# The end of a hybrid layer kernel: the last 64 tokens on all 128 partitions, and GpSimd as a third engine for the last block

## Chip, cores and metric

The kernel runs on one core of one Trainium2 chip. The metric is the device time of one execution in microseconds; lower is better. Three runs of the kernel before have a median of 1894.53 us.

## What is computed

One step of a one-layer streaming encoder, in fp32, for 320 tokens (64 of a sample, 256 of a prompt) of 2048 features: a projection, two attention mixers, a gated merge, a channel mixer with 8192 hidden features, a gated per-layer embedding and a final normalisation. Only the last two matter here:

```python
def rmsnorm(x, g):
    y = x32 * lax.rsqrt(jnp.mean(x32 * x32, axis=-1, keepdims=True) + RMS_EPS)
    return (y * g.astype(jnp.float32)).astype(x.dtype)
...
    gate = jax.nn.sigmoid(rmsnorm(h, g_ple) @ w_ple_gate)
    return h + (ple.astype(h.dtype) @ w_ple_proj) * gate
...
    y_prompt = rmsnorm(hp, g_final)
    y_sample = rmsnorm(hs, g_final)
```

## The kernel before

Activations lie transposed: features on the 128 partitions in 16 blocks (`KB`), 320 tokens (`TOK`) in the columns of each block. Every weight matrix comes as slabs of 8 x 128 x 128 over the SP queue, is split into a high and a low part by ACT (L628) and DVE (L947), and is multiplied in three passes (L394 to L396). The order on each engine is that of the code, with semaphores written out by hand.

The last matrix is the gate of the per-layer embedding, one block of 128 features after another. For each block, DVE scales the bank (L1131), ACT takes the sigmoid (L804), DVE multiplies by the projected embedding (L1245) and adds it to `h` (L1247); GpSimd squares the block (L1337) and adds it to `ssq` (L1340), and ACT multiplies `h` by the final gain (L913). The last block has code of its own, in two halves of 160 tokens: DVE L1258, ACT L922, then DVE L1262 (product), L1264 (sum) and L1269 (square). ACT loads the table of the square root meanwhile (L643) and scales the block by the gain (L925).

Then the result is turned into rows. TensorE sums the squares over the partitions for three groups of 128 tokens, 0 to 127, 128 to 255 and 192 to 319 (L596 for `ssq`, L604 for the last block's `sq`). ACT takes the root (L928), DVE the reciprocal (L1271). A "piece" is 128 tokens by 512 features: four transposes into a bank (L588), then a scaling by the reciprocal root out of the bank into `y_rows`, even pieces on ACT (L935), odd ones on DVE (L1278). There are five banks for pieces, and four pieces are transposed before the sums are known. The third group has only 64 new tokens. They come out on partitions 64 to 127 of their banks, and their pieces are scaled and stored as 64 rows. Two pieces make a store of 1024 features on the SP queue (L362): six stores, those of 128, 128 and 64 rows for the first half of the features, then the same for the second. SP waits for both engines' count of pieces before each, and at the end for all stores.

Two earlier transfers on ACT's queue are spoken of too. L747 copies a table from DRAM to DRAM into `bias_rows`, which is 1024 rows of 1 KB; L748 and L749, the `rolled` outputs, follow it as 16 pieces of 16 KB each. L774 and L775 each store 8 rows:

```python
act.dma_start(bias_rows, bass.AP(tensor=rel.tensor, offset=P - 1, ap=[[BIAS_ROW, HEADS], [-1, P], [1, 2 * P]])).then_inc(s_brow, 16)
act.dma_start(f_rows, f_sum[0:HEADS, :]).then_inc(s_fst, 16)
act.dma_start(io["logf_t"], logf[:, PAST:KEYS]).then_inc(s_out, 16)
```

The first view is (stride, count) by dimension, the outermost first: 8 heads, 128 rows, 256 elements. L963, also spoken of, is DVE's low part of an input block, `x_lo`, from `h` and `x_hi`.

## Time and profile before

| what | value |
|---|---|
| median of three runs | 1894.53 us (1893.93 to 1895.15) |
| the profiled execution, its own time | 1894.25 us |
| its span | 1892.4 us |
| TensorE busy | 1882.9 us |
| moved by DMA | 292.36 MB, mean 154 GB/s |

The span runs from the first to the last record of the profiled execution, and its own time is 1.85 us longer. All rows are from that one execution, in microseconds from the start of the span. PE is the matmul engine, DVE, ACT and POOL (GpSimd) are the others, SPq and ACTq are the queues of transfers that SP and ACT issue. A DMA share of 1.00 means that all 16 DMA engines of the core are busy (it can read a little over 1).

### The profile page before, as it was taken

The page shows a single profiled execution, that of the slowest core. Times are in us where ns is not written, and L with a number is a line of the kernel's source. Part 1 is how long each engine was busy: PE and PEld are TensorE (multiplying, and loading weights), DVE is VectorE, ACT ScalarE, POOL GpSimd, SP SyncE. Part 2 cuts the span into 40 slices and gives each one's busy share as a digit, 9 for nine tenths or more (in the row PEclk, how much of TensorE's full clock was granted, in tenths as well). Part 3 has the DMA queues.
Part 4 walks back from the last instruction along what each step waited for, and adds up shares of the span by engine and source line. Part 5 has one row for each costly group of instructions (what it writes and reads, how often), then busy time and mean ns, then how long its engine had stood idle before and what let it go on. Part 6 is the DMA issues. An engine that isn't in the chain of part 4 may idle for free.

```text
span 1892.4 us, 34998 instructions
## 1 busy us (share of the span) xinstructions
PE 1882.9 (99%) x12883; PEld 1879.1 (99%) x12883; DVE 894.3 (47%) x1122; ACT 726.8 (38%) x907; POOL 193.9 (10%) x280
## 2 busy tenths in 40 slices
PE   9999999999999999999999999999999999999998
PEld 9999999999999999999999999999999999999998
DVE  8544444444444444555443444444444344455544
ACT  6334443343333333334333333333333233333554
POOL 0111111120000000220100011000100001122121
PEclk9999999999999999999999999999999999999999
DMA  7544444546444444444444444444444444444442
GB/s 263 169 158 163 161 161 163 164 138 214 148 155 133 157 154 139 149 155 152 144 156 155 140 149 155 156 145 143 152 146 154 146 149 142 153 153 145 152 149 100
DMA packets 94306, 292.36 MB, mean 154 GB/s; under 512 B 13072, under 2 KB 26536, under 8 KB 94120
## 3 DMA queue, kind: packets, MB, share of 16 engines
q1 hardware_dynamic: 75760, 275.32, 44.3%
q10 hardware_dynamic: 18520, 16.69, 2.9%
q8 instruction: 17, 0.28, 0.1%
q14 instruction: 9, 0.07, 0.0%
HBM read 284.08 MB, written 9.46 MB: 155 GB/s over the span
## 4 chain that ended last, share of the span: by engine, by line
PE 99%; DVE 0%; DMA 0%; ACT 0%; issue 0%; SPq 0%; ACTq 0%
PE banks L394 31%; PE banks L396 31%; PE banks L395 31%; PE banks L470 0%; PE banks L471 0%; PE banks L472 0%; PE banks L416 0%; PE banks L419 0%; PE banks L417 0%; PE banks L568 0%; PE banks L566 0%; PE banks L567 0%; DMA h<-in_x_t 0%; PE banks L445 0%; PE banks L444 0%; PE banks L447 0%
## 5 line engine op out<-in xcount | busy, mean ns | idle before, releaser
L628 ACT ACTIVATE w_hi<-w_raw 128x1024 fp32r<-128x1024 f32 x510 | 539.7, 1061 | 996.4 <-PE banks L396 987.7
L394 PE MATMUL banks<-x_hi,w_hi 128*128 128x320 f32 x2512 | 780.6, 311 | 0.0
L396 PE MATMUL banks<-x_hi,w_lo 128*128 128x320 f32 x2512 | 776.2, 309 | 0.0
L395 PE MATMUL banks<-x_lo,w_hi 128*128 128x320 f32 x2512 | 776.1, 309 | 0.0
L947 DVE TENSOR_TENSOR w_lo<-w_raw,w_hi 128x1024 fp32r<-128x1024 f32 x510 | 605.0, 1222 | 23.7 <-ACT w_hi L628 23.6
L395 PEld LDWEIGHTS banks<-x_lo,w_hi 128*128 128x128 f32 x2512 | 471.8, 188 | 0.2
L394 PEld LDWEIGHTS banks<-x_hi,w_hi 128*128 128x128 f32 x2512 | 471.7, 188 | 0.2
L396 PEld LDWEIGHTS banks<-x_hi,w_lo 128*128 128x128 f32 x2512 | 471.6, 188 | 0.0
L394 PE MATMUL banks<-o_hi,w_hi 128*128 128x320 f32 x1280 | 395.6, 309 | 0.0
L396 PE MATMUL banks<-o_hi,w_lo 128*128 128x320 f32 x1280 | 395.5, 309 | 0.0
L395 PE MATMUL banks<-o_lo,w_hi 128*128 128x320 f32 x1280 | 395.5, 309 | 0.0
L394 PEld LDWEIGHTS banks<-o_hi,w_hi 128*128 128x128 f32 x1280 | 240.3, 188 | 0.0
L395 PEld LDWEIGHTS banks<-o_lo,w_hi 128*128 128x128 f32 x1280 | 240.3, 188 | 0.0
L396 PEld LDWEIGHTS banks<-o_hi,w_lo 128*128 128x128 f32 x1280 | 240.3, 188 | 0.0
L1174 DVE TENSOR_TENSOR h<-banks,h 128x320 f32 x80 | 39.4, 492 | 263.2 <-PE banks L396 263.2
L1348 POOL TENSOR_TENSOR tmp<-tmp 128x320 f32<-128x320 f32 x64 | 46.2, 722 | 741.5 <-DVE tmp L1188 741.5
L1188 DVE SCALAR_TENSOR_TENSOR tmp<-banks,rstd 128x320 f32<-128x320 f32 x64 | 31.5, 492 | 137.6 <-PE banks L396 137.6
L1337 POOL TENSOR_TENSOR sq<-h 128x320 f32 x47 | 33.9, 722 | 584.5 <-DVE h L1174 504.0
L1131 DVE TENSOR_TENSOR tmp<-banks,rstd 128x320 f32<-128x320 f32 x47 | 23.1, 491 | 126.6 <-PE banks L396 126.6
L1192 DVE TENSOR_TENSOR o_lo<-tmp,o_hi 128x320 f32 (+1 forms) x64 | 31.5, 492 | 104.7 <-ACT o_hi L860 103.4
L394 PE MATMUL banks<-m_hi,w_hi 128*128 128x320 f32 x256 | 79.1, 309 | 0.0
L395 PE MATMUL banks<-m_lo,w_hi 128*128 128x320 f32 x256 | 79.1, 309 | 0.0
(159 smaller groups left out, 1046.0 us busy)
## 6 DMA issues: line engine op xcount, KB each, us to landing
w_raw<-in_w_slabs SPq DMA_DIRECT2D x515, 512.0 KB, 4.1
out_kv_t<-k_t ACTq DMA_DIRECT2D x16, 160.0 KB, 3.7
out_kv_t<-v_t ACTq DMA_DIRECT2D x16, 160.0 KB, 4.4
h<-in_x_t ACTq DMA_DIRECT2D x1, 2560.0 KB, 10.2
out_y<-y_rows SPq DMA_DIRECT2D x4, 512.0 KB, 4.0
h<-in_x_t SPq DMA_DIRECT2D x3, 640.0 KB, 9.2
f_keys<-f_rows ACTq DMA_DIRECT2D x8, 224.0 KB, 3.1
bias_rows<-in_rel_rows ACTq DMA_DIRECT2D x1, 1024.0 KB
```

Of the source, the lines that this page charges most:

```text
L394: nc.tensor.matmul(out, w_hi[:, slot, ws], hi[:, xs], start=k == lo_k, stop=False)
L395: nc.tensor.matmul(out, w_hi[:, slot, ws], lo[:, xs], start=False, stop=False)
L396: mm = nc.tensor.matmul(out, w_lo[:, slot, ws], hi[:, xs], start=False, stop=k == hi_k)
L628: nc.scalar.activation(w_hi[:, slot, :], w_raw[:, slot, :], ACT.Copy).then_inc(s_whi, 1)
L947: nc.vector.tensor_tensor(w_lo[:, slot, :], w_raw[:, slot, :], f32(w_hi[:, slot, :]), ALU.subtract).then_inc(s_wlo, 1)
L1131: nc.vector.tensor_tensor(tm(dst), summed(t, base), rstd[:, :], ALU.mult).then_inc(s_acc, 1)
L1174: nc.vector.tensor_tensor(blk(h, n), summed(t), blk(h, n), ALU.add).then_inc(s_acc, 1)
L1188: nc.vector.scalar_tensor_tensor(out=tm(0), in0=acc, scalar=0.0, in1=rstd[:, :], op0=ALU.max, op1=ALU.mult).then_inc(s_acc, 1)
L1192: nc.vector.tensor_tensor(blk(o_lo, n), tm(1), f32(blk(o_hi, n)), ALU.subtract).then_inc(s_olo, 1)
L1337: nc.gpsimd.tensor_tensor(sq[:, :], blk(h, n), blk(h, n), ALU.mult).then_inc(s_sq, 1)
L1348: nc.gpsimd.tensor_tensor(tm(1), tm(0), tm(0), ALU.mult).then_inc(s_sqr, 1)
```

## The change

The third group of tokens gets all 128 partitions. For it, TensorE turns four blocks of the features' second half (all 128 columns, of which partitions 64 to 127 are wanted) and then, over partitions 0 to 63 of the same bank, the matching blocks of the first half for the 64 tokens alone. So there are ten pieces in place of twelve, all of 128 partitions by 512, and the third group is one store, whose target is seen as (half, token, feature). Its place is third, behind the first halves of the other groups. Since the token's reciprocal root is now wanted on partitions 0 to 63 too, DVE takes a second reciprocal that moves it there.

The last block is cut at 128 tokens in place of 160. GpSimd does product, sum and square for the first 128, DVE for the other 192, and GpSimd multiplies the whole block by the gain, which ACT did.

```diff
-Y_ROWS = ((0, 0, P), (P, 0, P), (TOK - P, P - (TOK - 2 * P), TOK - 2 * P))
+LAST_TOK = TOK - 2 * P
 Y_BLOCKS = 4
-Y_PIECES = tuple((rows, 2 * pair + e) for pair in range(KB // Y_BLOCKS // 2) for rows in range(len(Y_ROWS)) for e in range(2))
+HALF_KB = KB // 2
+Y_PIECES = ((0, 0), (0, 1), (1, 0), (1, 1), (2, 0), (2, 1), (0, 2), (0, 3), (1, 2), (1, 3))
+Y_COLS = (0, D_MODEL, 2 * D_MODEL)
...
-        def token_half(t, half):
-            return t[:, half * (TOK // 2):(half + 1) * (TOK // 2)]
+        def token_part(t, part):
+            return t[:, part * P:part * P + (P, TOK - P)[part]]
+        def tokens_of(t, rows, block=0):
+            last = block * TOK + min(rows * P + P, TOK)
+            return t[:, last - P:last]
         def y_piece(n, at_bank):
             rows, group = Y_PIECES[n]
-            first, at, count = Y_ROWS[rows]
-            cols = slice(group * Y_BLOCKS * P, (group + 1) * Y_BLOCKS * P)
+            first = Y_COLS[rows] + group * Y_BLOCKS * P
             if at_bank:
-                return banks[at:at + count, Y_BANKS[n % len(Y_BANKS)], 0:Y_BLOCKS * P]
-            return y_rows[at:at + count, rows * D_MODEL + cols.start:rows * D_MODEL + cols.stop]
+                return banks[:, Y_BANKS[n % len(Y_BANKS)], 0:Y_BLOCKS * P]
+            return y_rows[:, first:first + Y_BLOCKS * P]
...
-                first, at, count = Y_ROWS[rows]
                 cols = slice(group * Y_BLOCKS * P, (group + 2) * Y_BLOCKS * P)
-                src = y_rows[at:at + count, rows * D_MODEL + cols.start:rows * D_MODEL + cols.stop]
+                src = y_rows[:, Y_COLS[rows] + cols.start:Y_COLS[rows] + cols.stop]
+                dst = io["y"][rows * P:rows * P + P, cols] if rows < 2 else \
+                    io["y"][2 * P:TOK, :].rearrange("t (h c) -> h t c", h=2)
                 sp.wait_ge(s_scaled[0], pair + 1)
                 sp.wait_ge(s_scaled[1], pair + 1)
-                sp.dma_start(io["y"][first + P - count if at else first:first + P, cols], src).then_inc(s_stored, 16)
+                sp.dma_start(dst, src).then_inc(s_stored, 16)
...
             def turn_piece(n):
                 rows, group = Y_PIECES[n]
-                first = Y_ROWS[rows][0]
                 for j in range(Y_BLOCKS):
                     block = group * Y_BLOCKS + j
-                    src = h[:, block * TOK + first:block * TOK + first + P]
-                    tr = nc.tensor.transpose(banks[:, Y_BANKS[n % len(Y_BANKS)], j * P:(j + 1) * P], src, ident[:, :])
+                    out = banks[:, Y_BANKS[n % len(Y_BANKS)], j * P:(j + 1) * P]
+                    if rows < 2:
+                        tr = nc.tensor.transpose(out, tokens_of(h, rows, block), ident[:, :])
+                    else:
+                        nc.tensor.transpose(out, tokens_of(h, rows, block + HALF_KB), ident[:, :])
+                        tr = nc.tensor.transpose(out[0:LAST_TOK], tokens_of(h, rows, block)[:, P - LAST_TOK:P], ident[:, :])
                 tr.then_inc(s_turned_y, 1)
             ready_pieces = len(Y_BANKS) - 1
             pe.wait_ge(s_ssq, 3 * KB)
             row_sums = [banks[:, bank, 0:1] for bank in SUM_BANKS]
-            for out, (first, at, count) in zip(row_sums, Y_ROWS):
-                nc.tensor.matmul(out, ssq[:, first:first + P], ones[:, 0:1], start=True, stop=False)
+            for rows, out in enumerate(row_sums):
+                nc.tensor.matmul(out, tokens_of(ssq, rows), ones[:, 0:1], start=True, stop=False)
             pe.wait_ge(s_hg, KB - 1)
             for n in range(ready_pieces):
                 turn_piece(n)
-            for out, (first, at, count) in zip(row_sums, Y_ROWS):
-                pe.wait_ge(s_gated[3], 1 if first + P <= TOK // 2 else 2)
-                mm = nc.tensor.matmul(out, sq[:, first:first + P], ones[:, 0:1], start=False, stop=True)
+            for rows, out in enumerate(row_sums):
+                pe.wait_ge(s_squared[min(rows, 1)], 1)
+                mm = nc.tensor.matmul(out, tokens_of(sq, rows), ones[:, 0:1], start=False, stop=True)
             mm.then_inc(s_sum, 1)
             for n in range(ready_pieces, len(Y_PIECES)):
                 if n == len(Y_BANKS) - 1:
@@ -611,9 +626,9 @@
                     done = n - len(Y_BANKS)
                     pe.wait_ge(s_scaled[done % 2], by_engine(done + 1, done % 2))
-                if Y_PIECES[n][1] == KB // Y_BLOCKS - 1:
-                    pe.wait_ge(s_hg, KB)
+                if Y_PIECES[n] in ((0, 3), (1, 3), (2, 1)):
+                    pe.wait_ge(s_lasthg, 1)
...
-                nc.scalar.activation(token_half(tm(1), part), token_half(tm(0), part), ACT.Sigmoid).then_inc(s_gated[1], 1)
+                nc.scalar.activation(token_part(tm(1), part), token_part(tm(0), part), ACT.Sigmoid).then_inc(s_gated[1], 1)
             ready_root()
-            act.wait_ge(s_gated[3], 2)
-            nc.scalar.activation(blk(h, KB - 1), blk(h, KB - 1), ACT.Copy, scale=gain(FINAL, KB - 1)).then_inc(s_hg, 1)
             act.wait_ge(s_sum, 4)
             sums = banks[:, SUM_BANKS[0]:SUM_BANKS[-1] + 1, 0:1].rearrange("p b n -> p (b n)")
-            nc.scalar.activation(mean[:, 0:len(Y_ROWS)], sums, ACT.Sqrt, bias=eps[:, :], scale=1.0 / D_MODEL).then_inc(s_row_root, 1)
-            act.wait_ge(s_row_rstd, 1)
+            nc.scalar.activation(mean[:, 0:len(SUM_BANKS)], sums, ACT.Sqrt, bias=eps[:, :], scale=1.0 / D_MODEL).then_inc(s_row_root, 1)
             for n in range(0, len(Y_PIECES), 2):
                 rows = Y_PIECES[n][0]
-                first, at, count = Y_ROWS[rows]
+                if n == 0 or rows == 2:
+                    act.wait_ge(s_row_rstd, 1 + rows // 2)
                 act.wait_ge(s_turned_y, n + 1)
-                nc.scalar.activation(y_piece(n, False), y_piece(n, True), ACT.Copy, scale=rstd[at:at + count, rows:rows + 1]).then_inc(s_scaled[0], 1)
+                nc.scalar.activation(y_piece(n, False), y_piece(n, True), ACT.Copy, scale=rstd[:, rows:rows + 1]).then_inc(s_scaled[0], 1)
...
-                nc.vector.tensor_tensor(token_half(tm(0), part), token_half(acc, part), token_half(rstd, part), ALU.mult).then_inc(s_gated[0], 1)
-            for part in range(2):
-                dve.wait_ge(s_gated[1], part + 1)
-                nc.vector.tensor_tensor(token_half(tm(2), part), token_half(tm(1), part), token_half(blk(ple_part, n), part), ALU.mult).then_inc(s_gated[2], 1)
-                dve.wait_ge(s_gated[2], part + 1)
-                nc.vector.tensor_tensor(token_half(blk(h, n), part), token_half(blk(h, n), part), token_half(tm(2), part), ALU.add).then_inc(s_plep, 1)
-                dve.wait_ge(s_plep, KB + part)
-                if part == 0:
-                    dve.wait_ge(s_ssq, 3 * KB)
-                nc.vector.tensor_tensor(token_half(sq, part), token_half(blk(h, n), part), token_half(blk(h, n), part), ALU.mult).then_inc(s_gated[3], 1)
+                nc.vector.tensor_tensor(token_part(tm(0), part), token_part(acc, part), token_part(rstd, part), ALU.mult).then_inc(s_gated[0], 1)
+            dve.wait_ge(s_gated[1], 2)
+            nc.vector.tensor_tensor(token_part(tm(2), 1), token_part(tm(1), 1), token_part(blk(ple_part, n), 1), ALU.mult).then_inc(s_gated[2], 1)
+            dve.wait_ge(s_gated[2], 1)
+            nc.vector.tensor_tensor(token_part(blk(h, n), 1), token_part(blk(h, n), 1), token_part(tm(2), 1), ALU.add).then_inc(s_plep, 1)
+            dve.wait_ge(s_plep, KB)
+            dve.wait_ge(s_ssq, 3 * KB)
+            nc.vector.tensor_tensor(token_part(sq, 1), token_part(blk(h, n), 1), token_part(blk(h, n), 1), ALU.mult).then_inc(s_squared[1], 1)
             dve.wait_ge(s_row_root, 1)
-            nc.vector.reciprocal(rstd[:, 0:len(Y_ROWS)], mean[:, 0:len(Y_ROWS)]).then_inc(s_row_rstd, 1)
+            nc.vector.reciprocal(rstd[:, 0:len(SUM_BANKS)], mean[:, 0:len(SUM_BANKS)]).then_inc(s_row_rstd, 1)
             dve.wait_ge(s_row_rstd, 1)
+            nc.vector.reciprocal(rstd[0:LAST_TOK, 2:3], mean[LAST_TOK:P, 2:3]).then_inc(s_row_rstd, 1)
             for n in range(1, len(Y_PIECES), 2):
                 rows = Y_PIECES[n][0]
-                first, at, count = Y_ROWS[rows]
+                if n == 1 or rows == 2:
+                    dve.wait_ge(s_row_rstd, 1 + rows // 2)
                 dve.wait_ge(s_turned_y, n + 1)
-                nc.vector.tensor_scalar(y_piece(n, False), y_piece(n, True), rstd[at:at + count, rows:rows + 1], None, ALU.mult).then_inc(s_scaled[1], 1)
+                nc.vector.tensor_scalar(y_piece(n, False), y_piece(n, True), rstd[:, rows:rows + 1], None, ALU.mult).then_inc(s_scaled[1], 1)
         @block.gpsimd
@@ -1348,6 +1362,19 @@
                     nc.gpsimd.tensor_tensor(tm(1), tm(0), tm(0), ALU.mult).then_inc(s_sqr, 1)
             add_squares(1, s_acc, T_PLE - KB + 1)
             add_squares(2, s_hfin, 1, KB - 1)
+            n = KB - 1
+            pool.wait_ge(s_pread, 4)
+            pool.wait_ge(s_gated[1], 1)
+            nc.gpsimd.tensor_tensor(token_part(tm(2), 0), token_part(tm(1), 0), token_part(blk(ple_part, n), 0), ALU.mult).then_inc(s_gated[3], 1)
+            pool.wait_ge(s_gated[3], 1)
+            nc.gpsimd.tensor_tensor(token_part(blk(h, n), 0), token_part(blk(h, n), 0), token_part(tm(2), 0), ALU.add).then_inc(s_gated[3], 1)
+            pool.wait_ge(s_gated[3], 2)
+            nc.gpsimd.tensor_tensor(token_part(sq, 0), token_part(blk(h, n), 0), token_part(blk(h, n), 0), ALU.mult).then_inc(s_squared[0], 1)
+            for part in range(2):
+                pool.wait_ge(s_squared[part], 1)
+            nc.gpsimd.tensor_scalar(blk(h, n), blk(h, n), gain(FINAL, n), None, ALU.mult).then_inc(s_lasthg, 1)
```

On SP, the queue of stores, the end of the program read before:

```order
L330 DMA w_raw<-in_w_slabs 128x1024
L347 REGISTER_ALU
L347 COMPARE_AND_BRANCH
L362 DMA out_y<-y_rows 128x1024 [waits piece_scaled_vector,piece_scaled_scalar] x2
L362 DMA out_y<-y_rows 64x1024 [waits piece_scaled_vector,piece_scaled_scalar]
L362 DMA out_y<-y_rows 128x1024 [waits piece_scaled_vector,piece_scaled_scalar] x2
L362 DMA out_y<-y_rows 64x1024 [waits piece_scaled_vector,piece_scaled_scalar]
L124 UNCONDITIONAL_BRANCH [waits y_stored]
```

and reads now:

```order
L340 DMA w_raw<-in_w_slabs 128x1024
L357 REGISTER_ALU
L357 COMPARE_AND_BRANCH
L373 DMA out_y<-y_rows 128x1024 [waits piece_scaled_vector,piece_scaled_scalar] x2
L373 DMA out_y<-y_rows 2x64x1024 [waits piece_scaled_vector,piece_scaled_scalar]
L373 DMA out_y<-y_rows 128x1024 [waits piece_scaled_vector,piece_scaled_scalar] x2
L127 UNCONDITIONAL_BRANCH [waits y_stored]
```

Five stores stand where six stood, and the third has a target of three dimensions; its source is 128 partitions of 1024 elements.

On GpSimd, behind the loop that sums the squares, the program ended; now its end reads:

```order
L1351 TENSOR_TENSOR sq<-h 128x320
L1354 TENSOR_TENSOR ssq<-ssq,sq 128x320 [waits square_ready]
L1347 REGISTER_ALU
L1347 COMPARE_AND_BRANCH
L1369 TENSOR_TENSOR tmp<-tmp,ple_part 128x128 [waits last_block_gated1,ple_part_read]
L1371 TENSOR_TENSOR h<-h,tmp 128x128 [waits last_block_gated3]
L1373 TENSOR_TENSOR sq<-h 128x128 [waits last_block_gated3]
L1377 TENSOR_SCALAR h<-h,gains 128x320 [waits last_block_squared1,last_block_squared0]
L127 UNCONDITIONAL_BRANCH
```

Four operations are new there, each behind the one before it. On DVE the last block's part was two such triples:

```order
L1258 TENSOR_TENSOR tmp<-banks,rstd 128x160 [waits slab_multiplied]
L1258 TENSOR_TENSOR tmp<-banks,rstd 128x160
L1262 TENSOR_TENSOR tmp<-tmp,ple_part 128x160 [waits last_block_gated1]
L1264 TENSOR_TENSOR h<-h,tmp 128x160 [waits last_block_gated2]
L1269 TENSOR_TENSOR sq<-h 128x160 [waits square_sum_ready,ple_gated]
L1262 TENSOR_TENSOR tmp<-tmp,ple_part 128x160 [waits last_block_gated1]
L1264 TENSOR_TENSOR h<-h,tmp 128x160 [waits last_block_gated2]
L1269 TENSOR_TENSOR sq<-h 128x160 [waits ple_gated]
L1271 RECIPROCAL rstd<-mean 128x3 [waits row_roots_ready]
```

and is now one, with a second reciprocal behind it:

```order
L1272 TENSOR_TENSOR tmp<-banks,rstd 128x128 [waits slab_multiplied]
L1272 TENSOR_TENSOR tmp<-banks,rstd 128x192
L1275 TENSOR_TENSOR tmp<-tmp,ple_part 128x192 [waits last_block_gated1]
L1277 TENSOR_TENSOR h<-h,tmp 128x192 [waits last_block_gated2]
L1281 TENSOR_TENSOR sq<-h 128x192 [waits square_sum_ready,ple_gated]
L1283 RECIPROCAL rstd<-mean 128x3 [waits row_roots_ready]
L1285 RECIPROCAL rstd<-mean 64x1 [waits row_rstd_ready]
```

## Rows read from the trace of the kernel before

**Rows 1.** The page, parts 1 and 4: busy time, and the chain by engine

```profile
PE 1882.9 (99%) x12883; PEld 1879.1 (99%) x12883; DVE 894.3 (47%) x1122; ACT 726.8 (38%) x907; POOL 193.9 (10%) x280
...
PE 99%; DVE 0%; DMA 0%; ACT 0%; issue 0%; SPq 0%; ACTq 0%
```

**Rows 2.** Chain of waits at the end, in order of time: start us, us, what

```profile
1878.26 0.34 DVE tmp L1258
1878.62 0.35 ACT tmp L922
...
1880.67 0.34 DVE sq L1269
1881.05 0.62 PE banks L604 x4
...
1881.99 0.19 DVE rstd L1271
1882.20 0.70 ACT y_rows L935
...
1886.25 0.76 DVE y_rows L1278
```

**Rows 3.** Timeline of the SP queue, first and third store: start us, us, what

```profile
1883.03 0.35 SPq L362 DMA_DIRECT2D out_y<-y_rows  x1
...
1884.47 0.53 SPq L362 DMA_DIRECT2D out_y<-y_rows  x1
```

**Rows 4.** Windows of the tail: stretch, length, busy time by engine, PEclk, DMA share, GB/s

```profile
1883.75:1884.00 0.25, 0.25 (x5) 0.25 (x4) 0.25 (x1) 0.25 (x1) 0.00 (x0) 1.00 0.58 229
1884.00:1884.25 0.25, 0.25 (x5) 0.25 (x4) 0.25 (x1) 0.23 (x2) 0.00 (x0) 1.00 1.00 410
1884.00:1886.50 2.50, 2.21 (x21) 1.98 (x19) 2.14 (x4) 2.24 (x4) 0.00 (x0) 1.00 1.02 397
1886.50:1888.00 1.50, 0.00 (x0) 0.00 (x0) 0.51 (x1) 0.00 (x0) 0.00 (x0) 1.00 1.00 197
1891.25:1891.50 0.25, 0.00 (x0) 0.00 (x0) 0.00 (x0) 0.00 (x0) 0.00 (x0) 0.50 0.91 279
```

**Rows 5.** DMA view, 1883 to 1892 us: all packets of the six stores

```profile
DMA packets 736, 2.62 MB, mean 291 GB/s; under 512 B 96, under 2 KB 96, under 8 KB 736
```

**Rows 6.** DMA view, 52.2 to 54.1 us: queue 10, packets, MB, share

```profile
q10 hardware_dynamic: 32, 0.02, 6.6%
```

**Rows 7.** DMA view, 19 to 31.5 us: queue 10

```profile
q10 hardware_dynamic: 1096, 1.57, 41.1%
```

**Rows 8.** Timeline, 1872 to 1882 us, DVE, POOL and ACT

```profile
1872.78 0.49 DVE L1247 TENSOR_TENSOR h<-h,tmp 128x320 f32<-128x320 f32 x1
1873.54 0.72 POOL L1337 TENSOR_TENSOR sq<-h 128x320 f32 x1 [1.88 <-DVE h L1247]
...
1881.03 0.56 ACT L925 ACTIVATE h<-h,gains 128x320 f32<-128x320 f32 x1 [0.32 <-DVE sq L1269]
```

**Rows 9.** Groups of instructions by line and form: busy us, mean ns, idle before

```profile
L963 DVE SCALAR_TENSOR_TENSOR x_lo<-h,gains,x_hi 128x320 fp32r<-128x320 f32 x16 | 7.8, 550 | 1.3 <-ACT x_hi L722 1.3
L1247 DVE TENSOR_TENSOR h<-h,tmp 128x320 f32 x14 | 6.9, 493 | 1.7
L1264 DVE TENSOR_TENSOR h<-h,tmp 128x160 f32<-128x160 f32 x2 | 0.7, 326 | 0.1
L1340 POOL TENSOR_TENSOR ssq<-ssq,sq 128x320 f32<-128x320 f32 x47 | 41.4, 880 | 3.7
L1337 POOL TENSOR_TENSOR sq<-h 128x320 f32 x47 | 33.9, 722 | 584.5 <-DVE h L1174 504.0 <-DVE h L1247 80.5
L1313 POOL TENSOR_SCALAR probs<-probs,inv_sum 128x128 f32<-128x128 f32 x16 | 10.4, 648 | 285.8 <-DVE inv_sum L997 285.8
```

**Rows 10.** Timeline at 745 us: a GpSimd and a DVE operation at once

```profile
745.44 0.88 POOL L1340 TENSOR_TENSOR ssq<-ssq,sq 128x320 f32<-128x320 f32 x1
745.45 1.22 DVE L963 SCALAR_TENSOR_TENSOR x_lo<-h,gains,x_hi  x1 [1.09 <-ACT x_hi L848]
```

More of the change, by code:

```diff
@@ L148, in hybrid_layer @@
         wf = under("wf", [P, WF_COLS], F32R)
-        y_rows = under("y_rows", [P, len(Y_ROWS) * D_MODEL])
+        y_rows = under("y_rows", [P, 2 * D_MODEL + D_MODEL // 2])
         m_hi = sb("m_hi", [P, KB * TOK], F32R)
@@ L254, in hybrid_layer @@
         s_gated = [sem(f"last_block_gated{i}") for i in range(4)]
+        s_lasthg = sem("last_block_gained")
+        s_squared = [sem(f"last_block_squared{i}") for i in range(2)]
         s_root = sem("root_ready")
```

## The prediction

> **What bounds the kernel now.** Start with the busy shares and the chain that ended last: TensorE is busy for 1882.9 of 1892.4 us and holds 99% of the chain [rows 1]. Up to the last gate product at 1878.2 us nothing in the change touches anything, so the whole question lies in the last 14 us. There the chain in order of time [rows 2] shows a relay between DVE, ACT and PE: gate logits at 1878.26, sigmoid, product, sum and square in two halves of 160 tokens until 1881.01, row sums until 1881.67, root, reciprocal, and the first scaling at 1882.20. The SP queue's timeline [rows 3] shows the first of six stores issued at 1883.03, and the windows [rows 4] show its data flowing from about 1883.85 (a 0.58 share of the quarter from 1883.75) to about 1891.5. From there on the reader is to look at the DMA share, not at an engine: it stands near 1.00 all the way, while DVE and ACT are done at 1887.0. The tail is bound by the 16 DMA engines, 7.65 us of data, followed by 0.9 us to the end of the span.
>
> The windows also show two rates. With full stores running, 397 GB/s on average; in the stretch in which the first 64-partition store runs, 197 GB/s at the same busy share. So 256 KB from 64 partitions cost as much as 512 KB from 128: 512 KB at 410 GB/s, the best quarter [rows 4], are 1.28 us, and six stores are 6 x 1.28 = 7.68, which is the 7.65 read.
>
> **The change, part by part.**
>
> *Six stores become five.* Two stores of 64 partitions go, and one with 128 source partitions comes. The total is 2.62 MB, as before. If all 16 engines share it, it costs 1.28 us in place of 2.56.
>
> *How the new store is spread.* This is the term that decides. Its source is 128 partitions; its target is the view "h t c", whose outer dimension is 2, then 64 rows of 4 KB. The order rows show 2x64x1024 where all the others have 128x1024. How many engines share a store can be read from its completion packets of 4 bytes: one for each engine that took part. The six stores of the end left 96 of them, 16 each, for outer dimensions 128 and 64 [rows 5]. The two stores of 8 rows at 52 us (`f_rows`, `logf_t`) left 32 packets on queue 10 together: 16 rows of data and 16 completions, 8 each [rows 6]. The telling case is the copy into `bias_rows`: its target is 1024 rows, its source has an outer dimension of 8 and then 128. With the two `rolled` copies (16 pieces each) queue 10 moved 1096 packets: 1024 + 32 of data leaves 40 completions, 16 + 16 for `rolled` and 8 for `bias_rows` [rows 7]. The side with the small outer dimension decided, though the other side had 1024. A number of engines that divides both outer dimensions fits every one of these cases (16, 16, 8, 8), and for 128 against 2 it gives 2.
>
> The Trainium skill, "DMA: Bandwidth & Descriptors", section "Why a DMA increments its semaphore by 16 and not by 1", states this outright: the largest k up to 16 that divides the slowest non-size-1 dimension of both access patterns, on the lowest-numbered engines. By this rule the new store runs on two engines, and the trace agrees with its 8 completions for 8 against 1024.
>
> Price: one engine moves 410 / 16 = 25.6 GB/s, a 4 KB row in 0.16 us. The new store gives each of two engines 64 rows, 10.24 us. The same two carry a sixteenth of each of the other four stores, 4 x 1.28 = 5.12 us; the two ahead of it in their queue are before it, the two behind it wait. The other fourteen finish early and help nobody. The data phase is 5.12 + 10.24 = 15.36 us in place of 7.65: **+7.7 us**.
>
> *GpSimd takes 128 tokens of the last block.* DVE keeps 192. From 160 columns at 0.326 and 320 at 0.493 [rows 9] an operation of 192 is 0.36 us. GpSimd's for 128 columns is not in the trace: in proportion to 320 columns it is 0.29 to 0.35 (0.722 and 0.880 for one and two inputs), and its slowest kind, the scaling of 128x128, takes 0.648 [rows 9]. I take 0.40, near the first, since it is the same kind of operation. Both can start near 1879.1 (the first sigmoid is over by 1878.95 [rows 2], and a handoff: GpSimd took up DVE's block 0.27 us after its end at 1873.27 [rows 8]). Side by side they would be done near 1880.5, half a microsecond earlier than now. But they don't run side by side: DVE's `x_lo` operation on 320 columns takes 0.550 in the head of the kernel [rows 9] and 1.22 where a GpSimd operation of 0.88 runs: it starts at 745.45, 0.01 us after GpSimd's, and ends 0.35 us after it [rows 10]. So the six take turns: 3 x 0.40 + 3 x 0.36 = 2.3 us, to 1881.4, 0.4 us later than the 1881.01 of now.
>
> The Trainium skill, "SBUF — State Buffer", section "Who interferes with whom", has this as a lock: a DVE instruction with two SBUF inputs and a GpSimd instruction that reads SBUF exclude one another. By this rule the split gains nothing; the trace agrees with those 0.67 us of waiting.
>
> *Second reciprocal.* It moves rstd of partitions 64 to 127 to 0 to 63 and stands ahead of DVE's first scaling: 0.1 us by its like of 0.19 [rows 2], pipelined behind the first. *ACT's scaling of the last block* (0.56 us, over at 1881.59, before the sums [rows 2, 8]) moves to GpSimd: nothing on the path either way. On GpSimd it starts when both squares are there, about 1881.4, and is over by 1883.0 (1.6 at most, 320 columns in proportion to the 0.648); TensorE needs it for the second piece of the 64 tokens, which can't start before the first scaling is done, after 1883. *Transposes*: 48 before and after; *scalings*: 6 + 6 become 5 + 5. Their cover is the DMA queue, which is 4 us behind them already. The front costs **+0.4 us** in all; bounds: -0.2 with no waiting at all (six row-sum matmuls after the squares in place of four take back some), +1.6 if GpSimd needs 0.65 each and DVE waits for each.
>
> **Sum**: 1892.4 + 7.7 + 0.4 = 1900.5 of span. The profiled execution is 1894.25, 0.3 under the median of the runs, 1894.53; 1894.53 + 8.1 = **1902.6 us**. Measurements of this kernel tell a change from none at about 0.2%, 3.8 us; the forecast is twice that.
>
> **The rivals.**
>
> *A, sixteen engines* (ends not slower). If the side with 128 partitions decides, the store is 1.28 us: 6.4 in place of 7.65, with the front +0.4, gives 1894.53 - 1.25 + 0.4 = 1893.7. For it: no row has a small outer dimension on the target alone; in all three it is on the source or on both. Against: a store cut by one side's count must be cut so on the other too. The point of decision is the number of engines: 5.12 + 20.48 / k + 0.4 is 7.65 at k near 9.6; from 10 on it is no loss, 8 would cost 0.4. Chance 0.12.
>
> *B, SP is held.* Store issues lengthen as the queues fill (0.35 for the first, 0.53 for the third [rows 3]). With 64 rows in two queues SP may issue the fourth and fifth store only when those have emptied; each then adds the 0.8 us from issue to first data: up to +1.6, 1903.4 to 1904.2. Against: the fourth and fifth need only wait behind the third anyway. Chance 0.10.
>
> *C, half rate.* Should the two engines meet at one port, as the 64-partition stores did (197 GB/s, twice the time), the store takes 20.5 us, near 1913. Source halves 0 to 63 and 64 to 127 speak against it. Chance 0.02.
>
> **How the numbers follow.** The forecast has 0.75, B 0.10, A 0.12, C 0.02, and 0.01 is for a gain that I can't name. Faster 0.01, same 0.12 (A), slower 0.87. The range: the forecast with the front at its lower bound is 1902.0, less a run's scatter and a slightly better rate on lone engines, 1901.0; B and the slow front reach 1904.8. A and C stay out, 0.14, and the rest of the 0.2 is for misses at the edges.
>
> **What would show it.** The third store lands 10 us or more after its issue and leaves 2 completions of 4 bytes, so 66 in all in place of 80; the windows from about 1888 on show a DMA share near 0.12 and 51 GB/s; engines are idle for the last 12 us. GpSimd's operations last longer than 0.40 where DVE's overlap, and the first store is issued near 1883.4. I am wrong if the DMA share stays near 1.00 to the end and the span is under 1893, or if the first store comes before 1883.0.

## The result, and the profile after

The changed kernel takes **1903.47 us** (median of 6 runs, 1903.06 to 1904.68), the kernel before 1895.03 (6 runs beside them, 1893.93 to 1895.59): a ratio of 1.0047, interval 1.0037 to 1.0057. It is 8.4 us slower. The forecast was 1902.6 in a range of 1901.0 to 1904.8.

The profiled execution took 1903.46 us, its span is 1901.7, 9.2 longer than before (1901.66 against 1892.44). The busy shares and the chain of the page answer to [rows 1]:

```profile
PE 1883.6 (99%) x12883; PEld 1879.6 (99%) x12883; DVE 893.3 (47%) x1119; ACT 724.4 (38%) x905; POOL 195.7 (10%) x284
...
PE 99%; DMA 0%; DVE 0%; ACT 0%; issue 0%; SPq 0%; ACTq 0%
```

They don't show the change: every engine is as busy as before, within 2.4 us, and TensorE has 99% of the chain again. The windows of the tail (stretch, length, busy by engine, PEclk, DMA share, GB/s) show where the time is; they answer to [rows 4]:

```profile
1883.75:1884.00 0.25, 0.25 (x5) 0.25 (x4) 0.09 (x1) 0.06 (x1) 0.00 (x0) 1.00 0.70 279
1884.00:1885.00 1.00, 1.00 (x12) 1.00 (x10) 0.95 (x2) 0.69 (x1) 0.00 (x0) 1.00 1.03 418
...
1886.00:1887.00 1.00, 0.00 (x0) 0.00 (x0) 0.34 (x1) 0.00 (x0) 0.00 (x0) 1.00 0.93 340
1887.00:1888.00 1.00, 0.00 (x0) 0.00 (x0) 0.00 (x0) 0.00 (x0) 0.00 (x0) 1.00 1.00 360
...
1889.00:1890.00 1.00, 0.00 (x0) 0.00 (x0) 0.00 (x0) 0.00 (x0) 0.00 (x0) 0.50 0.48 152
1890.00:1891.00 1.00, 0.00 (x0) 0.00 (x0) 0.00 (x0) 0.00 (x0) 0.00 (x0) 0.50 0.16 57
...
1892.00:1900.00 8.00, 0.00 (x0) 0.00 (x0) 0.00 (x0) 0.00 (x0) 0.00 (x0) 0.50 0.13 51
```

From 1884 to 1889 the DMA engines are nearly full (0.93 at the least), as before. Then the share falls, and from 1891 to 1900.9 it stays near 0.13, which is two engines of sixteen, at 51 GB/s. No compute engine works after 1886.4. The DMA view of the same stretch, against [rows 5], has 66 packets under 512 B, the completion packets of four stores at 16 and one at 2 (the other 641 are the 640 rows of 4 KB and one instruction fetch, on which more at the end):

```profile
DMA packets 707, 2.64 MB, mean 141 GB/s; under 512 B 66, under 2 KB 66, under 8 KB 706
```

Timeline of the SP queue: stores one, two, three and five (start us, us, what), against [rows 3]; and SP's waits (who waits for whom: us, times, longest us), where the last wait for the stores was 3.5 us before:

```profile
1882.99 0.35 SPq L373 DMA_DIRECT2D out_y<-y_rows  x1
1883.64 0.34 SPq L373 DMA_DIRECT2D out_y<-y_rows  x1
1884.74 0.68 SPq L373 DMA_DIRECT2D out_y<-y_rows  x1
1886.41 0.75 SPq L373 DMA_DIRECT2D out_y<-y_rows  x1
```

```profile
SPq L127 <- DMA out_y<-y_rows: 14.1, 1, 14.1
```

SP is not held by the long store: it issues the last one 1.7 us behind it. It waits at the end instead.

The front of the tail, in the timeline of ACT, POOL and DVE, against [rows 2, 8]:

```profile
1878.62 0.63 ACT L937 ACTIVATE tmp<-tmp 128x128 f32<-128x128 f32 x2 [3.65 <-DVE tmp L1272]
1879.08 0.46 POOL L1369 TENSOR_TENSOR tmp<-tmp,ple_part 128x128 f32<-128x128 f32 x1 [3.83 <-ACT tmp L937]
1879.28 0.47 DVE L1275 TENSOR_TENSOR tmp<-tmp,ple_part 128x192 f32<-128x192 f32 x1 [0.43 <-ACT tmp L937]
1879.61 0.45 POOL L1371 TENSOR_TENSOR h<-h,tmp 128x128 f32<-128x128 f32 x1
1879.78 0.50 DVE L1277 TENSOR_TENSOR h<-h,tmp 128x192 f32<-128x192 f32 x1
1880.14 0.40 POOL L1373 TENSOR_TENSOR sq<-h 128x128 f32<-128x128 f32 x1
1880.32 0.44 DVE L1281 TENSOR_TENSOR sq<-h 128x192 f32<-128x192 f32 x1
...
1881.76 0.18 DVE L1283 RECIPROCAL rstd<-mean 128x3 f32<-128x3 f32 x1 [1.00 <-ACT mean L941]
1881.97 0.16 DVE L1285 RECIPROCAL rstd<-mean 64x1 f32<-64x1 f32 x1
```

The last square is done at 1880.76, where it was 1881.01 before, and the first store is issued at 1882.99 instead of 1883.03.

From here on the "data phase" runs from the start of the first to the end of the last 4 KB packet of `y` in the trace of DMA packets. For the kernel before that is 1883.88 to 1891.68, 7.8 us, a little more than the 7.65 that the prediction read from quarters of a microsecond. Windows of the kernel before:

```profile
1883.50:1883.87 0.37, 0.37 (x6) 0.37 (x4) 0.34 (x2) 0.37 (x1) 0.00 (x0) 1.00 0.00 0
...
1891.68:1892.40 0.72, 0.00 (x0) 0.00 (x0) 0.00 (x0) 0.00 (x0) 0.00 (x0) 0.50 0.00 0
```

So the 9.2 us of span are: front nothing (data from 1883.84, before 1883.88), data 17.1 us (to 1900.95) in place of 7.8, which is +9.3, and 0.71 us from the last data to the end in place of 0.76. The medians differ by less, 8.4, because the profiled execution of before was 0.8 us under its median.

### The profile page after: what moved, and what is told of

Read it like the earlier page. It is cut to its first block, busy times and chain, and to the rows that moved or that the text cites. A ratio compares the mean times of both kernels' runs of the same rounds, so it can differ in the third digit from the quotient of the medians.

```text
span 1901.7 us, 34999 instructions
## 1 busy us (share of the span) xinstructions
PE 1883.6 (99%) x12883; PEld 1879.6 (99%) x12883; DVE 893.3 (47%) x1119; ACT 724.4 (38%) x905; POOL 195.7 (10%) x284
## 4 chain that ended last, share of the span: by engine, by line
PE 99%; DMA 0%; DVE 0%; ACT 0%; issue 0%; SPq 0%; ACTq 0%
PE banks L406 31%; PE banks L405 31%; PE banks L407 31%; PE banks L481 0%; PE banks L482 0%; PE banks L483 0%; PE banks L427 0%; PE banks L430 0%; PE banks L428 0%; PE banks L579 0%; PE banks L577 0%; DMA h<-in_x_t 0%; PE banks L578 0%; PE banks L456 0%; PE banks L455 0%; PE banks L458 0%
## 5 line engine op out<-in xcount | busy, mean ns | idle before, releaser
L1202 DVE SCALAR_TENSOR_TENSOR tmp<-banks,rstd 128x320 f32<-128x320 f32 x64 | 31.5, 492 | 137.8 <-PE banks L407 137.8
L1206 DVE TENSOR_TENSOR o_lo<-tmp,o_hi 128x320 f32 (+1 forms) x64 | 31.5, 492 | 104.5 <-ACT o_hi L875 103.1
```

The lines of the kernel that those rows point to most:

```text
L1202: nc.vector.scalar_tensor_tensor(out=tm(0), in0=acc, scalar=0.0, in1=rstd[:, :], op0=ALU.max, op1=ALU.mult).then_inc(s_acc, 1)
L1206: nc.vector.tensor_tensor(blk(o_lo, n), tm(1), f32(blk(o_hi, n)), ALU.subtract).then_inc(s_olo, 1)
```

## The experiments

In this part "pieces" are the 4 KB packets of `y`, one row each, and "completions" the 4-byte packets. In the profiles of these kernels DVE's first operation on the last gate block starts anywhere from 1877.87 to 1878.72 us, though the stores changed here stand behind it. So the spans of single profiles are compared with that in mind, and the data phase by itself.

### How many engines: the outer dimension alone

The same source and the same number of bytes in every one, with only the target's view changed (the remark on the right is its shape). The order in which the rows meet DRAM changes with it, so the last 64 tokens' values land in other places.

```diff
-  io["y"][2 * P:TOK, :].rearrange("t (h c) -> h t c", h=2)
+  io["y"][2 * P:TOK, :].rearrange("t (h c) -> (t h) c", h=2)                                       # 128 x 1024
+  io["y"][2 * P:TOK, :].rearrange("t (h c) -> (t h) c", h=2).rearrange("(b a) c -> a b c", a=8)    # 8 x 16 x 1024
+  io["y"][2 * P:TOK, :].rearrange("t (h c) -> (t h) c", h=2).rearrange("(b a) c -> a b c", a=16)   # 16 x 8 x 1024
```

> The changed kernel, with the third store's target seen as 128 rows of 1024 one behind the other (outer dimension 128, as its source); the values of the last 64 tokens go to other places of the output than the reference has them, all else is as in the change. Theory (the count of engines divides both outer dimensions): 16 engines, 5 x 16 = 80 completions of 4 bytes in the tail, data for 6.4 us at some 400 GB/s, last data near 1890.3, span near 1891.2, so 1.2 us under the span of the kernel before (1892.4) and 10.5 under that of the change (1901.7). Rival (the source's 128 partitions had 16 engines all along and the store is slow for the 64 rows of the target that share DRAM rows): the same 4 KB pieces go to the same DRAM rows, so the span stays near 1901.

> As the change, but the third store's target is 8 x 16 x 1024, which can't be merged to fewer dimensions; the values of the last 64 tokens land in other places. Theory: 8 engines, 64 + 8 = 72 completions; each of these engines has 16 pieces of the store, 2.56 us, so 5.12 + 2.56 = 7.7 us of data, span near 1892.4, up to 1893 if pieces get in each other's way. Rival (a target of three dimensions is slow in itself, whatever its outer size): span near 1901 as in the change.

> As the change, but the third store's target is 16 x 8 x 1024; the values of the last 64 tokens land in other places. Theory: 16 engines, 80 completions, 6.4 us of data, span near 1891.2, no different from an outer dimension of 128. Rival (three dimensions are slow in themselves): near 1901. Rival (the count goes by the source alone, with the target's pieces cut afterwards): no difference between the outer sizes 2, 8 and 16, which the span of 1901.7 for 2 against these two decides.

The DMA views of the three, in that order, 1883 to 1892 us for the first and third, 1883 to 1895 for the second:

```profile
DMA packets 720, 2.62 MB, mean 291 GB/s; under 512 B 80, under 2 KB 80, under 8 KB 720
```

```profile
DMA packets 713, 2.64 MB, mean 220 GB/s; under 512 B 72, under 2 KB 72, under 8 KB 712
```

```profile
DMA packets 720, 2.62 MB, mean 291 GB/s; under 512 B 80, under 2 KB 80, under 8 KB 720
```

| target of the third store | completions | data phase | span | time, us |
|---|---|---|---|---|
| 2 x 64 x 1024 (the change) | 66 | 17.1 | 1901.7 | 1903.47 |
| 8 x 16 x 1024 | 72 | 10.6 | 1894.9 | 1896.67 (one run) |
| 16 x 8 x 1024 | 80 | 8.1 | 1892.7 | 1894.71 (one run) |
| 128 x 1024 | 80 | 6.6 | 1891.5 | 1893.72 (10 runs) |

With 128 rows the ratio to the kernel before is 0.9996 (0.9987 to 1.0006): the whole loss is gone, and it hung on how one target is written. The count of engines is 2, 8, 16, 16, as forecast from the rows of before. It isn't the whole cost, though, and here two expectations missed: the targets with 8 and 16 in front were to take 7.7 and 6.4 us of data. All three targets with three dimensions take 1.7 to 2.9 us more than their count of engines explains (5.12 + 10.24, + 2.56 and + 1.28 us would be 15.4, 7.7 and 6.4). The row of 8 is the least clean of them: its profile has an instruction fetch of 1.68 us on one DMA engine at 1883.74, as its data begins.

### The place of the store

```diff
-Y_PIECES = ((0, 0), (0, 1), (1, 0), (1, 1), (2, 0), (2, 1), (0, 2), (0, 3), (1, 2), (1, 3))
+Y_PIECES = ((0, 0), (0, 1), (1, 0), (1, 1), (0, 2), (0, 3), (1, 2), (1, 3), (2, 0), (2, 1))
```

> The change with the store of the last 64 tokens as the fifth instead of the third. On two engines it took 11.7 us in the changed kernel's trace, not the 10.24 of 64 pieces at 0.16: the missing 1.5 us fell in the time in which the other fourteen engines were still storing. Theory: two engines still carry 96 pieces, but the long store now begins at about 1889 when the others have nothing left, so it takes 10.3 us, 66 completions, last data near 1899.3, span near 1900.1. Rival (the pieces of this store are slow by themselves): it takes 11.7 us again, span 1901.5 or more. Rival (its place in the queue is what costs): span well under 1898.

1902.88 us (4 runs, 1902.60 to 1902.98), ratio 1.0042 (1.0026 to 1.0059), data phase 16.5 us. Counted back from the end, the last 64 rows of each of the two engines took 11.2 us (1889.27 to 1900.44), not the 10.3 of the theory, though the other engines had nearly nothing left. The same thing is seen in the store by itself, below. The data phase is 0.6 us shorter than in the change. That isn't shown to come from the place: the run without GpSimd further down has the long store third, like the change, and 16.6 us of data. Place is a minor matter at most, the two engines are the cause.

### The store alone, and what makes it long

The other four stores are left out, so those rows of `y` are not written.

```diff
-                sp.dma_start(dst, src).then_inc(s_stored, 16)
-            sp.wait_ge(s_stored, 16 * (len(Y_PIECES) // 2))
+                if rows == 2:
+                    sp.dma_start(dst, src).then_inc(s_stored, 16)
+            sp.wait_ge(s_stored, 16)
```

> Only the third store is issued, the one with the target (half, token, feature); the other four are left out, so the rows of the first two groups are not written. Theory (two engines, 64 rows each at 0.16 us, and slow pieces come from the other stores): 10.2 to 10.3 us from its first to its last data, 2 completions, no piece over 0.2 us. Rival (the store is slow by itself, reading its two halves of partitions at once or starting late on each row): 11 to 12 us and slow pieces here as well.

> Only the third store is issued, with the plain target of 128 rows; the other four are left out, and the values of the last 64 tokens go to other places of their rows. Control for the next run and for the lone store on two engines: 16 engines, 8 rows each, 16 completions, every piece 0.16 to 0.18 us, 1.3 us from first to last data. If rows of any store come slowly at its start, as on two engines, some of its 128 pieces take 0.3 us or more and the data lasts over 1.6 us.

> Only the third store is issued, with the target of outer dimensions 16 x 8 x 1024; the other four are left out, and the values of the last 64 tokens go to other places. Theory (with three dimensions each engine takes rows of neighbouring partitions, and the 16 engines meet inside this one store): pieces of 0.30 to 0.37 us here too, 2.4 to 3 us from first to last data, 16 completions. Rival (they meet the rows of the stores around it): pieces of 0.16 to 0.18 us and 1.3 us, as in the control.

The lone store on two engines takes 11.3 us from first to last data (1886.45 to 1897.73) and leaves 2 completions. The rival has it: its rows come slowly by themselves. Timeline of SP and windows of this kernel:

```profile
1885.20 0.65 SPq L374 DMA_DIRECT2D out_y<-y_rows  x1
```

```profile
1887.00:1888.00 1.00, 0.00 (x0) 0.00 (x0) 0.00 (x0) 0.00 (x0) 0.00 (x0) 1.00 0.11 33
1888.00:1889.00 1.00, 0.00 (x0) 0.00 (x0) 0.00 (x0) 0.00 (x0) 0.00 (x0) 1.00 0.13 33
1889.00:1890.00 1.00, 0.00 (x0) 0.00 (x0) 0.00 (x0) 0.00 (x0) 0.00 (x0) 0.65 0.15 41
...
1896.00:1897.00 1.00, 0.00 (x0) 0.00 (x0) 0.00 (x0) 0.00 (x0) 0.00 (x0) 0.50 0.13 53
```

The same two engines move 33 GB/s at first and 53 later. In the packets it is a pattern: of the first 16 rows of each engine the third, fourth, eighth, twelfth and sixteenth take 0.30 to 0.58 us, on both engines at the same moment, and nearly all others 0.16; from 1890.3 on all take 0.16.

The two that use all 16 engines, alone, show the same without the count of engines. First the store of 128 rows: its issue, and the windows of its data:

```profile
1884.84 0.35 SPq L374 DMA_DIRECT2D out_y<-y_rows  x1
```

```profile
1885.50:1886.00 0.50, 0.13 (x2) 0.00 (x0) 0.38 (x2) 0.42 (x1) 0.00 (x0) 1.00 0.65 262
1886.00:1886.50 0.50, 0.00 (x0) 0.00 (x0) 0.42 (x1) 0.00 (x0) 0.00 (x0) 1.00 1.06 434
1886.50:1887.00 0.50, 0.00 (x0) 0.00 (x0) 0.00 (x0) 0.00 (x0) 0.00 (x0) 1.00 0.87 352
```

and that of 16 x 8 x 1024:

```profile
1884.79 0.63 SPq L374 DMA_DIRECT2D out_y<-y_rows  x1
```

```profile
1886.00:1886.50 0.50, 0.00 (x0) 0.00 (x0) 0.37 (x1) 0.00 (x0) 0.00 (x0) 1.00 0.92 221
1886.50:1887.00 0.50, 0.00 (x0) 0.00 (x0) 0.00 (x0) 0.00 (x0) 0.00 (x0) 1.00 1.05 188
1887.00:1887.50 0.50, 0.00 (x0) 0.00 (x0) 0.00 (x0) 0.00 (x0) 0.00 (x0) 1.00 0.80 197
1887.50:1888.00 0.50, 0.00 (x0) 0.00 (x0) 0.00 (x0) 0.00 (x0) 0.00 (x0) 1.00 1.06 426
```

128 rows: 1.4 us, no piece over 0.17. 16 x 8 rows: 2.1 us, issue 0.63 in place of 0.35 us, first data 1.28 us after the start of the issue in place of 0.85. The theory said 2.4 to 3 us, with slow pieces throughout because the engines meet in neighbouring partitions; but the pieces are slow (0.28 to 0.45) only in the first 1.3 us, and then run at 0.16, though the rows are still neighbours. So that reason is doubtful, and what slows the start of such a store stays open. The two kernels differ in the order of the rows in DRAM as well as in the number of dimensions, and no run separates the two. The price is shown, in one profile each: 0.7 us of data on 16 engines, 1.0 on two (11.3 against 10.24), and 0.4 before the first byte.

### The third store as two

```diff
...
+                else:
+                    for half in range(2):
+                        part = slice(half * LAST_TOK, (half + 1) * LAST_TOK)
+                        sp.dma_start(dst[half], src[part, :]).then_inc(s_stored, 16)
...
```

> The changed kernel with the third store cut in two of 64 partitions and 64 target rows each. If the count of engines is set by the outer dimension: all 16 engines share each, 96 completions, and each costs the 1.28 us of a 64-partition store of the kernel before, so the data phase is 7.65 to 7.8 us, the span 1892.3 and the time within 0.1% of the kernel before. Rival (stores that leave from all 128 partitions at once would meet differently): 64-partition stores of different halves follow one another on the same engines and overlap at their borders, data phase near 6.6 and 1893.4.

1894.67 us (10 runs), ratio 1.0002 (0.9992 to 1.0011), 96 completions, data phase 8.2 us. That is the time of the kernel before again, with two stores of 64 partitions on 16 engines each; the data phase is 0.4 us longer than its 7.8. The half rate of [rows 4] is here too: the second and third window below together are 213 GB/s at a share of 0.98. Windows:

```profile
1884.00:1886.00 2.00, 1.44 (x14) 1.20 (x12) 1.83 (x3) 1.38 (x2) 0.00 (x0) 1.00 1.00 401
...
1886.50:1887.00 0.50, 0.00 (x0) 0.00 (x0) 0.00 (x0) 0.00 (x0) 0.00 (x0) 1.00 1.25 287
1887.00:1887.50 0.50, 0.00 (x0) 0.00 (x0) 0.00 (x0) 0.00 (x0) 0.00 (x0) 1.00 0.71 139
```

The rival's 6.6 us did not come: using the two halves of the partitions one after the other does not help.

### GpSimd's part taken back

```diff
+            for part in range(2):
+                dve.wait_ge(s_gated[1], part + 1)
+                nc.vector.tensor_tensor(token_part(tm(2), part), token_part(tm(1), part), token_part(blk(ple_part, n), part), ALU.mult).then_inc(s_gated[2], 1)
...
+            nc.scalar.activation(blk(h, KB - 1), blk(h, KB - 1), ACT.Copy, scale=gain(FINAL, KB - 1)).then_inc(s_lasthg, 1)
-            nc.gpsimd.tensor_tensor(token_part(tm(2), 0), token_part(tm(1), 0), token_part(blk(ple_part, n), 0), ALU.mult).then_inc(s_gated[3], 1)
...
-            nc.gpsimd.tensor_scalar(blk(h, n), blk(h, n), gain(FINAL, n), None, ALU.mult).then_inc(s_lasthg, 1)
```

> The changed kernel with GpSimd's new work undone: DVE does product, sum and square for both parts of the last block (128 and 192 tokens), ACT multiplies the block by the gain, as before the change. The stores are the changed kernel's. Theory (the two parts take turns on GpSimd and DVE, but only partly: 1.68 us for the six operations; DVE alone needs 3 x 0.29 + 3 x 0.36 = 1.95 and a few hundredths between them): the squares are done near 1881.1, 0.3 later than in the changed kernel, the first store is issued near 1883.2, the span is 1901.9 to 1902.0. Rival (they took turns in full and GpSimd's operations are the slow ones): the squares are done by 1880.8 and the first store is issued by 1883.0 or earlier, and GpSimd brings nothing. The data phase is 17 us in both.

Timeline, the start of the sigmoid, DVE's first and last operation of the block, and the first of the five stores:

```profile
1878.20 0.63 ACT L937 ACTIVATE tmp<-tmp 128x128 f32<-128x128 f32 x2 [3.64 <-DVE tmp L1276]
1878.54 0.29 DVE L1281 TENSOR_TENSOR tmp<-tmp,ple_part 128x128 f32<-128x128 f32 x1
...
1880.18 0.36 DVE L1288 TENSOR_TENSOR sq<-h 128x192 f32<-128x192 f32 x1
...
1882.76 3.91 SPq L373 DMA_DIRECT2D out_y<-y_rows  x5
```

This execution started the sigmoid 0.42 us sooner, so what counts is the distance from the sigmoid: last square done 2.34 us after its start, first store issued 4.56 after. In the changed kernel: 2.14 and 4.37. GpSimd's help is worth 0.19 us, where 0.3 was expected. Read without that earlier start, the times would have been the rival's (squares by 1880.8, first store by 1883.0). The time is 1902.77 us in one run, so nothing was lost that can be seen. The data phase is 16.6 us where 17 was expected, though its stores are those of the change: which rows come slowly differs from one profile to the next.

### A version that keeps the idea and loses the cost

The last 64 tokens are laid out beforehand by ACT, while TensorE is busy, with the two halves of each token on neighbouring partitions (row 2t + half). Their store is then 128 rows in DRAM order, one transpose serves a block in place of two, no reciprocal moves across partitions, and the third group's sum and root come behind those of the other two.

```diff
-                    io["y"][2 * P:TOK, :].rearrange("t (h c) -> h t c", h=2)
+                    io["y"][2 * P:TOK, :].rearrange("t (h c) -> (t h) c", h=2)
...
+            blocks = h[:, :].rearrange("p (n t) -> p n t", t=TOK)[:, :, 2 * P:TOK]
+            laid = h_late.rearrange("p (n t e) -> p e n t", e=2, t=LAST_TOK)
+            nc.scalar.activation(laid[:, 0], blocks[:, 0:HALF_KB], ACT.Copy).then_inc(s_late, 1)
+            nc.scalar.activation(laid[:, 1, 0:HALF_KB - 1], blocks[:, HALF_KB:KB - 1], ACT.Copy).then_inc(s_late, 1)
```

> The same idea with a plain target: the last 64 tokens are laid out with the two halves of each token on neighbouring partitions (row 2t + half), by copies of ACT while TensorE is busy, so that their store is 128 rows of 1024 in DRAM order and no reciprocal moves across partitions; the third group's sums, root and reciprocal come behind those of the other two. Theory: 80 completions, data phase 6.4 to 6.6 us in place of 17.1, first store at 1882.8 to 1883.0, span near 1891.0, median 1893.1 to 1893.7, that is 0.04% to 0.07% under the kernel before, at the edge of what can be measured. Rival (the added small operations of ACT and DVE stand on the path ahead of the first scaling): the first store comes at 1883.4 or later and the time is that of the kernel before or up to 0.5 us more.

> The interleaved kernel again, unchanged, as the pair of the next one and to see whether its 1.8 us hold on another set of runs: 1892.4 to 1893.2, ratio to the kernel before 0.9985 to 0.9995. If the first measurement was luck, the ratio is within 0.03% of 1.

> The interleaved kernel with the other half of the change undone: DVE does product, sum and square for both parts of the last block, ACT the gain. Theory (GpSimd's help is worth the 0.19 us that separate 2.34 from 2.15 us between the first sigmoid and the last square): 0.2 to 0.3 us more than its pair from the first sigmoid to the first store, the same data phase of 6.6 us, and times that can't be told apart (difference of medians under 0.5 us). Rival (GpSimd's part brings what the layout seems to bring): the time returns to that of the kernel before, 1894.4 or more.

First set: **1892.76 us** (11 runs, 1892.20 to 1894.10), before 1894.60, ratio 0.9990 (0.9981 to 0.9999). Second set: 1893.08 against 1894.53, ratio 0.9993 (0.9984 to 1.0002). Without GpSimd: 1892.95, ratio 0.9992 (0.9983 to 1.0001). So the medians are 1.5 to 1.8 us lower, and the first set's is below the 1893.1 to 1893.7 that was expected, as its first store came 0.2 us ahead of the expected stretch. That is at the edge of what can be measured, since only the first set's interval leaves out 1; and GpSimd's part can't be seen in the time. Timeline and windows of the first set's profile:

```profile
1878.63 0.31 ACT L959 ACTIVATE tmp<-tmp 128x128 f32<-128x128 f32 x1 [2.28 <-DVE tmp L1297]
...
1882.58 4.20 SPq L390 DMA_DIRECT2D out_y<-y_rows  x5
```

```profile
1884.00:1889.00 5.00, 0.89 (x9) 0.65 (x6) 1.56 (x3) 1.01 (x2) 0.00 (x0) 1.00 1.01 404
1889.00:1889.50 0.50, 0.00 (x0) 0.00 (x0) 0.00 (x0) 0.00 (x0) 0.00 (x0) 1.00 1.00 410
1889.50:1890.00 0.50, 0.00 (x0) 0.00 (x0) 0.00 (x0) 0.00 (x0) 0.00 (x0) 1.00 0.80 303
```

The sigmoid starts when it did before (1878.62 [rows 2]), the first store is issued 0.45 us sooner, the data takes 6.6 us in place of 7.8 at a steady 404 GB/s, and these two, 0.45 and 1.2, are the 1.6 by which the span is less (1890.8). Without GpSimd the first store comes 4.14 us after the sigmoid's start (1878.54 to 1882.68) in place of 3.95: the 0.19 us again.

## Why the prediction was right, and where a term was off

*The decision.* Two engines for the third store: right. 66 completions, a share of 0.13 and 51 GB/s for the last 10 us of data, and the three other views of the same target move the count to 8 and 16. The Trainium skill's rule ("DMA: Bandwidth & Descriptors", section "Why a DMA increments its semaphore by 16 and not by 1") fits all four.

*Data phase, forecast +7.7, measured +9.3.* The term was mis-sized. It took a lone engine to move a row in 0.16 us from its first row on. Alone, the store takes 11.3 us, not 10.24, since some of its first rows are slow. Put last, the phase is 16.5, near 5.12 + 11.3. In the third place it is 17.1 in the change and 16.6 in the run without GpSimd, with the same five stores. So up to 0.6 us of the change's phase are slow rows that come in one profile and not in another; why was not separated further. The base was read 0.15 us short as well, 7.65 for 7.8, and 6 x 1.28 = 7.68 falls short of it too.

*Front, forecast +0.4, measured about 0.* The six operations of GpSimd and DVE take 1.68 us (1879.08 to 1880.76), not 2.3. DVE is slowed: its 192 columns take 0.44 to 0.50 us beside GpSimd and 0.35 to 0.36 alone, and its ends follow GpSimd's by 0.20 to 0.22 us three times over. (GpSimd took 0.40 to 0.46; no run has these operations of it alone.) But the next GpSimd operation has begun by then, so the durations may not be added. The step that failed is the sum 3 x 0.40 + 3 x 0.36. It was built on the one pair at 745 us [rows 10], and that pair did not show it: DVE ended 0.35 us behind GpSimd's operation, less than the 0.55 that its own takes, so the two together took 1.23 us and not 0.88 + 0.55. The Trainium skill's lock ("SBUF — State Buffer", section "Who interferes with whom") is borne out as a slowing. What the prediction drew from it, that the split gains nothing, holds but for 0.19 us. The second reciprocal costs 0.19 us for DVE's first scaling, not 0.1 (it starts at 1882.16, ACT's at 1881.97); ACT's isn't touched.

*Sum.* The two errors, +1.6 and -0.4, leave the span at 1901.7 for a forecast of 1900.5. The median is 0.9 over the forecast. That it is so near is in part luck: the errors have opposite signs, and without the front's +0.4 the forecast would have been 1.3 under. The mechanism and the count of engines were right.

*Rivals.* A (sixteen engines) is out by the 66 completions. Its price came out for another target: with 128 rows the median is 1893.72, where 1893.7 was worked out. Part of that is luck too, since the sum has the same +0.4 at the front. B (SP is held) is out: the last store is issued at 1886.41, 1.7 us behind the third. Its range of 1903.4 to 1904.2 holds the measured time all the same, by the wrong reason. C (half rate) is out: after the start two engines move 51 to 53 GB/s, 26 each.

*Signs.* All those of the data phase came; the store issued near 1883.4 did not. It came at 1882.99, 0.01 us below the bound named as a sign of error, and the error it points to is that of the front.

## What to carry to other kernels

Before a store's shape is changed, look at the outer dimension of both its sides, not at its bytes or its partitions: a small one puts all of it on that many engines, and the busy shares of the page won't show it. The completion packets of the DMA view count the engines, and the share in the last windows shows them. How many rows come slowly at the start of such a store has to be measured: that was the term the forecast had too low. If two halves must lie on different partitions, lay them out so that the target is a plain run of rows, even if that takes copies on an idle engine: here a few copies ahead of the end changed 17.1 us of data into 6.6.

## What the runs showed that was not expected

The targets of three dimensions cost more than their count of engines, even on all 16: issue 0.63 in place of 0.35 us, first data after 1.28 in place of 0.85, and 2.1 in place of 1.4 us of data for 512 KB, with slow pieces only in the store's first 1.3 us. Whether it is the dimensions or the order of the rows in DRAM was not tested.

One fetch of instructions may set the end. In the profile of the interleaved version without GpSimd (1894.9 us, where its median is 1892.95), a packet of 16 KB took 1.03 us of a DMA engine at 1885.92. DMA view of that kernel, and windows of its end:

```profile
q8 instruction: 1, 0.02, 0.6%
```

```profile
1889.00:1890.00 1.00, 0.00 (x0) 0.00 (x0) 0.00 (x0) 0.00 (x0) 0.00 (x0) 0.72 1.01 406
...
1890.25:1891.00 0.75, 0.00 (x0) 0.00 (x0) 0.00 (x0) 0.00 (x0) 0.00 (x0) 0.50 0.07 27
1891.00:1892.00 1.00, 0.00 (x0) 0.00 (x0) 0.00 (x0) 0.00 (x0) 0.00 (x0) 0.50 0.07 29
```

Fifteen engines have finished at 1890.2; one, at a share of 0.07, ends at 1892.3, 2.1 us behind, with 13 rows left that it moved at 0.16 us each. That it is the one which fetched is inferred from this lag, since the packets don't name their engine, and the fetch itself accounts for only half of it. The lag is as large as the whole gain of that version, so a single profile can hide the gain. The change's profile has such a fetch too (1.11 us at 1886.93). It did not set the end there, since a third engine, which finished at 1890.9 when the other thirteen were done by 1889.8, seems to have carried it.
